# A decoder step whose input projection is woven with a recurrence: VectorE's subtraction for the next tile's low weights stands 2.9 k-steps later in VectorE's program

## The reference, cut to what matters

```python
h = x * (1.0 + sc_m) + sh_m
q_a, kvc, kvs, kvw, g_a, p_b, q_c, k_c, v_c, g_mrg = _split(h @ lp['w_in'], IN_SPLITS)
...
o_b, new['rwkv'], new['rwkv_shift'] = rwkv7_mix(p_b, shift0, S0, lp)
```

## Time and profile before

| | |
|---|---|
| median of the runs (lowest, highest) | 1933.16 us (1930.5, 1934.42) |
| the profiled execution, its span | 1922.61 us, 1920.8 us |
| mean granted TensorE clock in it | 0.954 of 2.4 GHz |
| TensorE busy | 1722.9 us, 90% of the span |
| VectorE busy | 1100.5 us, 57% |
| ScalarE, GpSimd busy | 569.5 us, 425.6 us |
| matmuls of the projection | from 52.4 to 718.9 us |

### The profile page before, as it was taken

One profiled execution on the slowest core, in us unless ns is written; L12 is line 12 of the kernel. 1 busy time (PEld: TensorE's weight loads), 2 busy tenths in 40 slices (PEclk: granted clock), 3 DMA queues, 4 the chain that ended last, 5 costly groups with the idle time before them and its releaser, 6 DMA issues. The chain is left out here.

```text
span 1920.8 us, 38852 instructions
## 1 busy us (share of the span) xinstructions
PE 1722.9 (90%) x16171; PEld 1506.5 (78%) x16171; DVE 1100.5 (57%) x1937; ACT 569.5 (30%) x1216; POOL 425.6 (22%) x525
## 2 busy tenths in 40 slices
PE   4999888988989995999998997777899999999998
PEld 1898778887988994999986454554797999999776
DVE  3214676677665433899974555364586544444456
ACT  1235433333222321343433665222553200000000
POOL 0000910000001303232312779544100000000500
PEclk7899999998999997999997999898999999999999
DMA  5547774353444766665653852567574233333231
GB/s 230 158 127 208 183 230 147 108 175 106 156 145 160 241 213 224 216 217 186 219 147 131 308 141 83 170 232 250 182 215 147 77 88 89 88 88 135 88 98 70
DMA packets 241285, 311.14 MB, mean 162 GB/s; under 512 B 41557, under 2 KB 192493, under 8 KB 235222
## 3 DMA queue, kind: packets, MB, share of 16 engines
q1 hardware_dynamic: 211862, 176.72, 30.0%
q0 software_dynamic: 29248, 131.93, 21.2%
HBM read 281.19 MB, written 79.61 MB: 188 GB/s over the span
## 5 line engine op out<-in xcount | busy, mean ns | idle before, releaser
L302 PE MATMUL inp_acc<-hh,inp_wh 128*128 128x272 f32 (+1 forms) x1072 | 340.1, 317 | 20.8 <-DVE inp_wl L274 18.8
L302 PE MATMUL inp_acc<-hl,inp_wh 128*128 128x272 f32 (+1 forms) x1072 | 316.2, 295 | 0.0
L302 PE MATMUL inp_acc<-hh,inp_wl 128*128 128x272 f32 (+1 forms) x1072 | 316.0, 295 | 0.0
L302 PEld LDWEIGHTS inp_acc<-hh,inp_wh 128*128 128x128 f32 (+1 forms) x1072 | 207.1, 193 | 36.2 <-DVE inp_wl L274 19.3
L274 DVE TENSOR_TENSOR inp_wl<-inp_w,inp_wh 128x1024 fp32r<-128x1024 f32 (+1 forms) x67 | 81.2, 1212 | 233.6 <-ACT inp_wh L455 233.2
L302 PEld LDWEIGHTS inp_acc<-hl,inp_wh 128*128 128x128 f32 (+1 forms) x1072 | 208.3, 194 | 3.4 <-issue 3.1
L302 PEld LDWEIGHTS inp_acc<-hh,inp_wl 128*128 128x128 f32 (+1 forms) x1072 | 207.6, 194 | 0.4
L563 POOL DMA_DIRECT2D out_dram<-in_cache_dil_dram x84 | 42.8, 514 | 519.2 <-PE inp_acc L302 498.5
L1410 PE MATMUL cmp_pH<-cmp_RTh,cmp_w1h 128*128 128x256 f32 (+1 forms) x512 | 150.1, 293 | 3.4 <-issue 3.4
L269 DVE CAST trk_wh<-trk_w 128x1024 fp32r<-128x1024 f32 x62 | 46.4, 749 | 180.3 <-PE trk_pz L283 124.2
L1410 PE MATMUL cmp_pH<-cmp_RTl,cmp_w1h 128*128 128x256 f32 (+1 forms) x512 | 147.2, 287 | 0.4 <-issue 0.4
(11 more groups left out here) (597 smaller groups left out, 3805.5 us busy)
## 6 DMA issues: line engine op xcount, KB each, us to landing
inp_w<-in_w_in_dram SPq DMA_DIRECT2D x66, 512.0 KB, 6.1
trk_w<-in_w_ffn_dram SPq DMA_DIRECT2D x66, 512.0 KB, 3.9
out_dram<-in_cache_dil_dram POOLq DMA_DIRECT2D x64, 511.0 KB, 5.5
sdi_kv<-in_cache_dil_dram SPq DMA_DIRECT2D x288, 64.0 KB
ringA<-in_w_ada_dram SPq DMA_DIRECT2D x16, 1024.0 KB, 7.5
PT<-inp_o SPq DMA_DIRECT2D x58, 272.0 KB, 4.7
ada_wada<-in_w_ada_dram SPq DMA_DIRECT2D x8, 1024.0 KB, 17.6
out_dram<-in_cache_dil_dram POOLq DMA_DIRECT2D x16, 508.0 KB, 8.2
```

Of the source, the lines that this page charges most:

```text
L302: i = pe.matmul(out, l, r, start=(first and n == 0), stop=(last and n == 2))
```

## The change

The subtraction of tile n is put down at `at(n - 1, 2.5)` and no longer at `at(n - 1, -0.4)`: in VectorE's program it stands 2.9 k-steps (0.906 positions) later among the mixer's operations, behind those with positions in between. For tiles up to 14 `at` leaves out k, so that their positions stay. For tiles 15 to 66, 52 in all, it moves. What it computes, waits for and signals is the same, and no other engine's program changes.

```diff
     def vector(self, dve):
         for n, (c, t, rows) in enumerate(self.tiles):
-            yield self.at(n - 1, -0.4) if n else self.at(0) - 0.9
+            yield self.at(n - 1, 2.5) if n else self.at(0) - 0.9
             dve.wait_ge(self.high, n + 1)
             split_low(dve, self.wl[:, n % 2, :, 0:rows], self.w[:, n % self.NW, :, 0:rows], self.wh[:, n % 2, :, 0:rows]).then_inc(self.low, 1)
```

## The result

The changed kernel takes 1899.17 us (median of four runs, 1896.13 to 1902.35) against 1931.83 us for the kernel before in the same comparison (1927.21 to 1934.42): ratio 0.9834, 95% interval 0.9804 to 0.9863, 26 to 38 us faster. The forecast was 1906, 27.1 us faster, with a range of 1893 to 1928. The profiled executions lie 20.7 us apart (spans 1920.8 and 1900.1 us), less than the medians: the one before (1922.6 us) was 9 us faster than its median, the one after (1901.9 us) 3 us slower than its own.

What follows compares the result with a forecast made beforehand. TensorE was taken to bound 190 to 720 us, with 48 us idle, mostly waiting for VectorE's mixer operations. 25.4 + 7.5 - 2.85 - 3 = 27.1 us faster, 1906 us against the 1933.16 median, range 1893 to 1928.

Steps and rivals of the forecast that it cites:

- the walk: TensorE's waits taken one by one against VectorE's new order: which operations now precede the subtraction; 25.4 us won after 243 us.
- The sum of the terms after 243 us: TensorE's waits after 243 us that shrink or go: 9.7 + 1.6 + 4.0 + 4.4 + 5.7 = 25.4 us.
- new places: Eight tiles where the subtraction now stands ahead of L979, L983 or L973: 0 to 23 us lost, 3 taken.
- L923: TensorE's eight waits there for L985, 18.5 us: six lose 9.7 together, the other two 1.6.
- The two long runs: VectorE runs behind L923's waits of 3.18 us at 457.7 and 4.47 at 474.4: only 0.45 and 1.15 won.
- the first wait: L923's wait of 4.03 us for L985: loses 1.79 of standstill and 1.15 of subtraction, 2.9 us.
- L745, L1015, L1105, L1010: TensorE waits after 243 us, all to go: L745 for L881 4.0 us, L1015 2.2, L1105 1.7, L1010 1.2.
- L903 for L968: TensorE's 3.2 us wait: nothing won, as tile 38's subtraction leaves that VectorE run but tile 37's enters it.
- The fixed point: Near 241 us L1207 waits for DMAs: gains ahead of it are lost, plus 1.15 us subtraction and 1.7 low clock, -2.85.
- The clock: 1.2 GHz stretches behind five waits that go, up to 8.5 us: 7.5 us taken as won.
- the clock of the stretch is 0.98: Sign to look for: TensorE's mean granted clock in the projection's stretch, 0.96 before, becomes 0.98.
- The cover: Subtraction stands 5.5 k-steps, some 7.8 us, ahead of TensorE's need; with a largest lag of 3 us, it holds.

Runs made afterwards that it cites:

- Experiments 1 and 2: Subtraction moved only for the 17 tiles named by the walk: 1899.95 us, ratio 0.9823 against the kernel before; only for the other 35: 1926.08 us, ratio 0.9973.
- experiment 9: experiment 4 plus the subtractions of tiles 26 and 27 at k-step 6 and tile 38 at k-step 4: 1883.8 us, ratio 0.9735 against the kernel before.
- experiment 11: The changed kernel measured and profiled again with no edit: 1901.16 us, ratio 0.9834 against the kernel before.
- Experiment 3: Subtraction moved only for tiles 15 to 24, ahead of the point that DMA fixes: 1935.8 us, ratio 1.0015 against the kernel before.
- experiment 4: The changed kernel with the sample recurrence starting two positions later, so L1207 no longer stands ahead of L973: 1888.24 us, ratio 0.9762 against the kernel before.
- experiment 8: The changed kernel with the subtraction at k-step 7.4 of the tile before instead of 2.5: 1920.95 us, ratio 0.9928 against the kernel before.
- k-step 1.0: The changed kernel with the subtraction at k-step 1.0 of the tile before instead of 2.5: 1894.84 us, ratio 0.9808 against the kernel before.
- k-step 4.0: The changed kernel with the subtraction at k-step 4.0 of the tile before instead of 2.5: 1899.86 us, ratio 0.9817 against the kernel before.
- k-step 6.0: The changed kernel with the subtraction at k-step 6.0 of the tile before instead of 2.5: 1890.09 us, ratio 0.9769 against the kernel before.
- experiment 10: The changed kernel with all 52 subtractions at k-step 6.0 and the sample recurrence two positions later: 1893.26 us, ratio 0.9767 against the kernel before.

## Why the prediction was right

**The subtraction in front of an operation that TensorE needed was the cause.** Experiments 1 and 2 show it: the 17 tiles that the walk named carry the gain, the other 35 nearly nothing. The sum of the terms after 243 us, 25.4 less 3 for new places, 22.4 us of idle time, stands against 22.0 measured. The single terms are less exact, and their errors cancel in part:

- L923: 7.2 us should stay, before new places; 8.9 stayed, 2.45 of them at a new place (below). The two long runs keep 0.85 and 3.75 us, where I had 2.7 and 3.3; the first wait kept 0.96 of the forecast 1.1; one near 364 us that should have gone kept 0.94.
- L745, L1015, L1105, L1010: all gone behind 243 us, as forecast.
- L903 for L968: forecast to stay at 3.2, as tile 37's subtraction enters the run that tile 38's leaves. It did, in two parts, 1.06 at L963 and 2.05 at L968, 3.1 together. The changed kernel's rows, VectorE and then TensorE:

```profile
400.30 0.69 DVE L1141 TENSOR_TENSOR rw_sq<-obT 128x512 f32<-128x512 f32 x1
400.91 1.22 DVE L274 TENSOR_TENSOR inp_wl<-inp_w,inp_wh 128x1024 fp32r<-128x1024 f32 x1
```
```profile
412.39 0.39 PE L903 MATMUL rw_B<-rw_kkf,rw_kp 64*64 64x64 f32 x4 [2.05 <-DVEq L968]
```

- New places: 3 us were taken and 4.1 came: 2.45 at L923 (tile 26's subtraction in front of L979, below; experiment 9 brought it to 1.15), and 1.65 at L728, where TensorE now comes earlier.

```profile
270.40 1.22 DVE L274 TENSOR_TENSOR inp_wl<-inp_w,inp_wh 128x1024 fp32r<-128x1024 f32 x1
271.54 0.69 DVE L979 TENSOR_TENSOR rw_early<-rw_early,rw_masks 128x512 f32<-128x512 f32 x1
```
```profile
277.64 0.35 PE L923 MATMUL rw_B<-rw_early 64*64 64x64 f32 x5 [2.45 <-DVE rw_TT L985]
```

**The fixed point.** L1207 did wait for its DMAs, tile 24's subtraction did come between it and L973, and the gain ahead of it was taken back. In the changed kernel, GpSimd, VectorE and TensorE, for the earlier trace rows:

```profile
237.14 0.56 POOL L1190 DMA_DIRECT2D rws_vs<-DQ  x1
```
```profile
240.34 1.22 DVE L1207 TENSOR_TENSOR rws_stmp<-rws_sS,rws_sq_ 128x1024 f32<-128x1024 f32 x1 [6.91 <-DMA rws_vs<-DQ]
241.60 1.22 DVE L274 TENSOR_TENSOR inp_wl<-inp_w,inp_wh 128x1024 fp32r<-128x1024 f32 x1
242.74 0.68 DVE L973 TENSOR_TENSOR rw_arb<-rw_B,rw_masks 128x512 f32<-128x512 f32 x1
```
```profile
243.57 0.60 PE L903 MATMUL rw_B<-rw_rr,rw_kp 64*64 64x64 f32 x12 [6.16 <-DVE rw_arb L973]
```

The 1.15 us showed as 0.4, since L1207 could start 0.7 us earlier in this execution; in experiment 11 it started at 241.26 and the point was 1.3 us later than before. Experiment 3 shows the mechanism by itself, experiment 4 that taking the point away wins time, of which at most about 10 us are the point's.

**The clock was mis-sized.** The prediction had +7.5 for stretches that vanish and -1.7 for one that appears, 5.8 in all. The five stretches behind the removed waits did vanish. But the one that appeared at the fixed point was long, and so was one that was left, behind L968, which the prediction had at nothing. TensorE alone at the lower level, in the changed kernel from 243 us on:

```profile
243.60:251.90 8.30, 8.30 (x62) 0.50 0.96 311
279.20:282.60 3.40, 3.40 (x17) 0.50 0.67 154
412.40:426.00 13.60, 13.60 (x133) 0.50 0.28 99
460.10:470.40 10.30, 6.55 (x50) 0.50 0.00 0
```

In the kernel before, the same list has nine stretches. The one behind the wait of 3.19 us for L968 and the sum of all nine:

```profile
423.00:426.40 3.40, 3.40 (x53) 0.50 0.56 169
sum 34.00, PE 33.23; mean PE 3.69
```

So TensorE was busy at the lower level for 33.2 us before and 31.9 after. Half of the difference, 0.7 us, is what the clock gave in this pair, where 5.8 were forecast, and the sign "the clock of the stretch is 0.98" did not come: it stayed at 0.96. A wait of 6.2 us was followed by 8.3 us at the lower level and not 3.4, and one of 2.05 us by 13.6. In the second execution of the changed kernel the sum is 19.7 us; the term varies by more than its forecast from one execution to the next. The sum without it, which the prediction gives as 19.6, is nearer to the pair's 20.7 than 27.1 is, though not because the removed waits had no low clock behind them.

**The cover.** At 2.5 TensorE's weight loads waited for `inp_wl` once, 0.2 us, where it was 0.3 before: as forecast. The lag of at most 3 us, which the prediction took for the cost of a missing cover, wasn't tested there; at 7.4 a wait of 6.2 us came, twice as long: the subtraction then stands behind a long run of the mixer (its rows are above, in experiment 8).

**The number.** Against the medians the forecast is 5 to 6 us too small (27.1 against 32.7 and, the second time, 31.8), within the interval of the ratio. Against the profiled pair, for which it was worked out, it is 6.4 us too large (27.1 against 20.7): 3.1 us in TensorE's busy time, where the clock's 5.8 were expected and 2.7 came, 3.6 in the later stages and 0.4 in idle time, less 0.75 at the point. So the mechanism and the idle time were right, and that the whole came near the medians is luck in part: why the two profiled executions lie off their medians, by 12 us together, isn't settled.

## What to carry to other kernels

An engine that works through its queue in order, and isn't the bound by its busy share, can still hold up the one that is: look for its longest wait by total time, and then for what stands behind it in the queue. Here that was 147.2 us in front of operations whose delay cost TensorE some 22 us. Moving the waiting instruction behind the operation that the bounding engine needs is enough; how much standstill is left says little. Go through the waits of the bounding engine one by one, with the new order written out, and look for a wait whose end is fixed by something that doesn't move: what is won ahead of it is won only if that goes too. Compare idle time and busy time apart: in two executions of the changed kernel the idle time agreed within 0.1 us, the busy time within 4.6.

## What the runs showed of the hardware that was not expected

The time at the 1.2 GHz level behind a wait of TensorE varies a lot, in the same place and after nearly the same wait. Behind the wait for L968, in seven of these traces:

| kernel | wait, us | then at a granted clock of 0.50, us |
|---|---|---|
| the changed kernel | 2.05 | 13.6 |
| k-step 1.0 | 1.98 | 13.6 |
| k-step 4.0 | 2.04 | 13.7 |
| k-step 6.0 | 2.00 | 10.2 |
| experiment 9 | 2.05 | 10.2 |
| experiment 10 | 2.00 | none |
| experiment 4 | 2.06 | none |

TensorE was busy through each of these stretches. Where there was none, the 12 us behind the wait ran at full clock, as in experiment 4:

```profile
406.15 0.35 PE L903 MATMUL rw_B<-rw_kkf,rw_kp 64*64 64x64 f32 x9 [2.06 <-DVEq L968]
```
```profile
407.30:419.30 12.00, 10.45 (x153) 1.00 0.34 89
```

The length of the wait alone does not decide, and what does isn't shown here. A price of 1.7 us for each is a low estimate: 13.6 us at half speed cost 6.8. Behind another wait, of 3.5 to 4 us near 152 us, the stretch lasted 3.4 us in the kernel before and in the changed one, 10.2 in experiment 4 and 13.6 in experiment 3.
